# Normalised rows turned by matmuls with a diagonal, and a first weight piece in three transfers

## The reference

```python
h = rms_norm(x, g_mix)                      # x * rsqrt(mean(x*x) + 1e-5) * g
proj = h @ w_in + b_in                      # 1024 -> 1024+256+256+3*1024+2*1024
q, k, v, cb, cc, cx, ga, gc = split(proj)
y_attn = sliding_window_attention(rope(q), rope(k), v, sinks) @ w_attn_o
y_conv = (cb * causal_short_conv(cc * cx, w_conv)) @ w_conv_o
x = x + (sigmoid(ga) * y_attn + sigmoid(gc) * y_conv) @ w_out
h = rms_norm(x, g_ffn)
x = x + moe(h)        # top 4 of 32 experts, each w_gate, w_up, w_down of 1024x1024
return rms_norm(x, g_final)
```

## Time and profile before

| | |
|---|---|
| runs | 1164.71 us median of 3 (1164.37 to 1169.08) |
| profiled execution | 1164.72 us, of which the span in the trace is 1162.9 us |
| busy share of the span | PE 96%, PE weight load 45%, DVE 31%, ACT 21%, POOL 2% |
| DMA | 447.44 MB, mean 385 GB/s over the span |
| chain that ended last | PE 69%, DMA 29% |

### The profile page before, as it was taken

How to read it: one execution, slowest core, us unless ns; L and a number is a source line. 1 busy time by engine, 2 the same in 40 slices (tenths; PEclk the granted TensorE clock), 3 DMA queues, 4 the chain that set the end, 5 groups by cost and what they waited for, 6 DMA issues and landing times.

```text
span 1162.9 us, 14215 instructions
## 1 busy us (share of the span) xinstructions
PE 1120.3 (96%) x5623; PEld 522.5 (45%) x5623; DVE 359.9 (31%) x684; ACT 238.9 (21%) x426; POOL 26.9 (2%) x59
## 2 busy tenths in 40 slices
PE   8999999999999999999999999999999999999997
PEld 7888888973333333333333333333333333333332
DVE  6988896742111121121111111111111111111111
ACT  6676765421000001000100000000000000000002
POOL 2100000000000000000000000000000000000000
PEclk9999999999999999999999999999999999999999
DMA  9455749899999999999999999999999999999995
GB/s 293 155 176 169 263 142 352 299 405 427 427 427 431 431 431 429 429 430 432 429 432 432 431 431 430 432 431 432 429 432 429 432 431 431 429 432 431 425 423 240
DMA packets 65393, 447.44 MB, mean 385 GB/s; under 512 B 4569, under 2 KB 44853, under 8 KB 46421
## 3 DMA queue, kind: packets, MB, share of 16 engines
q1 hardware_dynamic: 65088, 446.93, 92.9%
q10 hardware_dynamic: 277, 0.12, 0.0%
HBM read 445.59 MB, written 1.05 MB: 384 GB/s over the span
## 4 chain that ended last, share of the span: by engine, by line
PE 69%; DMA 29%; ACT 0%; DVE 0%; issue 0%; POOL 0%; ACTq 0%; DVEq 0%; POOLq 0%
PE psum L821 36%; DMA ring<-in_w_up 29%; PE psum L538 10%; PE psum L542 5%; PE psum L836 4%; PE psum L759 4%; PE psum L558 2%; PE psum L849 1%; PE psum L767 1%; PE psum L792 1%; PE psum L608 0%; PE psum L843 0%; PE psum L598 0%; PE psum L524 0%; PE psum L865 0%; PE psum L652 0%
## 5 line engine op out<-in xcount | busy, mean ns | idle before, releaser
L821 PE MATMUL psum<-ring,work 128*64 128x512 f32 x3072 | 694.9, 602 | 29.0 <-DMA ring<-in_w_up 28.5
L821 PEld LDWEIGHTS psum<-ring,work 128*64 128x64 f32 x3072 | 217.4, 138 | 456.3 <-issue 404.1
L1512 DVE TENSOR_SCALAR work<-psum 128x512 f32<-128x512 f32 x32 | 22.1, 692 | 280.7 <-PE psum L821 280.7
L538 PE MATMUL psum<-hh,w 128*128 128x512 f32 x384 | 97.4, 395 | 0.0
L1256 DVE TENSOR_TENSOR w<-ring,w 128x1024 fp32r<-128x1024 f32 x74 | 90.4, 1264 | 8.4 <-ACT w L1005 8.1
L1517 DVE TENSOR_SCALAR work<-psum 128x512 f32<-128x512 f32 x32 | 22.1, 692 | 205.7 <-PE psum L821 205.7
L1165 ACT COPY work<-psum 128x512 f32<-128x512 f32 x32 | 18.8, 587 | 311.2 <-PE psum L849 311.1
L1005 ACT CAST w<-ring 128x1024 fp32r<-128x1024 f32 x74 | 74.2, 1048 | 28.3 <-PE psum L542 15.2
L538 PEld LDWEIGHTS psum<-hh,w 128*128 128x128 f32 x384 | 68.9, 189 | 15.0 <-ACT w L1005 1.3
L1535 DVE TENSOR_TENSOR work<-psum,g2k 128x256 f32<-128x256 f32 x62 | 23.4, 419 | 165.5 <-PE psum L767 165.5
L1174 ACT ACTIVATE work<-work 128x512 f32<-128x512 f32 x32 | 20.2, 630 | 225.9 <-DVE work L1512 225.9
(11 more groups left out here) (210 smaller groups left out, 687.9 us busy)
## 6 DMA issues: line engine op xcount, KB each, us to landing
ring<-in_w_gate SPq DMA_DIRECT2D x25, 4096.0 KB, 39.7
ring<-in_w_up SPq DMA_DIRECT2D x25, 4096.0 KB, 37.2
ring<-in_w_down SPq DMA_DIRECT2D x25, 4096.0 KB, 39.9
ring<-in_w_gate SPq DMA_DIRECT2D x13, 2048.0 KB, 12.9
ring<-in_w_up SPq DMA_DIRECT2D x13, 2048.0 KB, 12.5
ring<-in_w_in SPq DMA_DIRECT2D x25, 1024.0 KB, 5.0
ring<-in_w_down SPq DMA_DIRECT2D x8, 2048.0 KB, 13.1
ring<-in_w_down SPq DMA_DIRECT2D x10, 1024.0 KB, 35.6
```

The lines of the kernel that those rows point to most:

```text
L538: pe.matmul(bank(b[m]).rearrange("p (x t) -> p x t", x=2), wH[:, par, m, k, :], both[:, :, k, :], start=(k == 0), stop=(k == KB - 1))
L821: mm = pe.matmul(psum[64 * h:64 * h + 64, b, :], src[:, k, :], w[:, k2, h * 512:(h + 1) * 512], start=(bias_of is None and k == 0), stop=( ...
```

## The change

What it does, part by part:

- `normed` is no longer made for the first norm. VectorE multiplies the 128 x 128 identity by 1/rms instead, once for each tile of tokens (`diag`), and TensorE multiplies the blocks of x itself by that diagonal: one float32 matmul both scales and turns a block. Five blocks (`LEAD`) of the first tile go ahead of the wait for the second diagonal; the other three stand between blocks of the second tile.
- `WARM` goes from 3 to 2.
- The first weight piece comes in three transfers (blocks 0 and 1, 2 and 3, 4 to 7), with a semaphore more.
- Its blocks 0 and 1 are rounded by VectorE ahead of the first `hL`, 2 and 3 by GpSimd ahead of 4 to 7; ScalarE rounds none of them.

```diff
-WARM = 3
+WARM = 2
+LEAD = 5
@@ names
+        diag = work[:, 0:TT * P].rearrange("p (t c) -> p t c", t=TT)
@@ SyncE
-            for half, full in enumerate((first_in, piece_full[0])):
-                ks = slice(4 * half, 4 * half + 4)
+            for k0, k1, full in ((0, 2, first_in), (2, 4, second_in), (4, KB, piece_full[0])):
+                ks = slice(k0, k1)
@@ TensorE, turn_normed
-                for t in range(TT):
-                    for k in range(KB):
-                        if k % 2 == 0:
-                            pe.wait_ge(normed_ready, 4 * t + k // 2 + 1)
-                        tr = pe.transpose(turned(k)[:, t * P:(t + 1) * P], normed[:, t, k * P:(k + 1) * P], ident)
-                        if t == TT - 1 and (k == 0 or k % 2):
-                            tr.then_inc(done, 1)
+                def scaled(t, k):
+                    return pe.matmul(turned(k)[:, t * P:(t + 1) * P], xres[:, t, k * P:(k + 1) * P], diag[:, t, :],
+                                     start=True, stop=True)
+
+                pe.wait_ge(diag_ready, 1)
+                for k in range(LEAD):
+                    scaled(0, k)
+                pe.wait_ge(diag_ready, 2)
+                for k in range(KB):
+                    tr = scaled(1, k)
+                    if k == 0 or k % 2:
+                        tr.then_inc(done, 1)
+                    if k + LEAD < KB:
+                        scaled(0, k + LEAD)
@@ ScalarE
-            act_e.wait_ge(first_in, 16)
-            nc.scalar.copy(*first_weights(0, 2)).then_inc(first_high, 1)
@@ VectorE
-                for quarter in range(4):
-                    at = slice(quarter * PW, (quarter + 1) * PW)
-                    v.tensor_scalar(normed[:, t, at], xres[:, t, at], small[:, 4 + t:5 + t], None, ALU.mult).then_inc(normed_ready, 1)
-                    if t == 0 and quarter == 0:
-                        mean_rows_in(1)
+                v.tensor_scalar(diag[:, t, :], ident, small[:, 4 + t:5 + t], None, ALU.mult).then_inc(diag_ready, 1)
                 if t == 0:
+                    mean_rows_in(1)
...
             dve.wait_ge(par_ready, 1)
+            dve.wait_ge(first_in, 16)
+            v.tensor_copy(*first_weights(0, 2)).then_inc(first_high, 1)
             for k in range(KB):
-                if k == 2:
-                    dve.wait_ge(first_in, 16)
-                    v.tensor_copy(*first_weights(2, 4)).then_inc(second_high, 1)
@@ GpSimd
+            pool.wait_ge(second_in, 16)
+            g.tensor_copy(*first_weights(2, 4)).then_inc(second_high, 1)
             pool.wait_ge(piece_full[0], 16)
```

More of the change, by code:

```diff
@@ L258, in hybrid_block @@
         quarter_full, quarter_used = sem("quarter_full"), sem("quarter_used")
-        first_in, second_high, rest_high = sem("first_in"), sem("second_high"), sem("rest_high")
+        first_in, second_in, second_high, rest_high = sem("first_in"), sem("second_in"), sem("second_high"), sem("rest_high")
         x_in = [sem(f"x_in{t}") for t in range(TT)]
@@ L266, in hybrid_block @@
         dve_step, act_step, pool_step = sem("dve_step"), sem("act_step"), sem("pool_step")
-        ssq_ready, ms_ready, rstd_ready, normed_ready = (sem("ssq_ready"), sem("ms_ready"), sem("rstd_ready"),
-                                                         sem("normed_ready"))
+        ssq_ready, ms_ready, rstd_ready, diag_ready = (sem("ssq_ready"), sem("ms_ready"), sem("rstd_ready"),
+                                                       sem("diag_ready"))
         par_turned, par_ready, x_turned, hT_ready = sem("par_turned"), sem("par_ready"), sem("x_turned"), sem("hT_ready")
```

## The result

The changed kernel takes 1167.57 us (median of 14 runs, 1165.65 to 1172.40); the kernel before, 1165.88 us (14 runs, 1163.95 to 1169.68). The ratio is 1.0023, 95% interval 1.0014 to 1.0032: slower by about 2.7 us (the two medians alone lie 1.7 us apart), where I had forecast 0.25 us, but within the 0.5% that I called no change.

| | spans, mean of n | largest span | outside the span, median |
|---|---|---|---|
| before (118 runs beside the experiments) | 1163.5 | 1166.8 | 1.85 |
| changed (22 runs) | 1165.7 ± 0.4 | 1169.6 | 2.7 |

What follows compares the result with a forecast made beforehand. TensorE was taken to bound the first 60 us, DMA of expert weights to set the pace from about 579 us. Span 1162.9 + 0.25 for TensorE's shift + 1.82 around it gave 1165.0 us, range 1163.8 to 1167.8.

Steps and rivals of the forecast that it cites:

- rival 2: TensorE's clock rises before 6.9 us, blocks end at 10.8, first product starts at 10.9; 1164.4 us; chance 0.2.
- The rival of four transposes' price: A float32 matmul of 128 columns costs four transposes, 0.44 us; first product 2.6 us later, 1167.6 us; chance 0.05.
- my 2.2: Ratio of a float32 block's estimated price to a transpose's, 0.24 / 0.109 us, at the upper clock.
- 6.40 us: End of the two idle matmuls at the start, instead of 8.11 us with three.
- I put the rise at 8.2: TensorE's clock goes up at 8.2 us, so about three blocks cost 0.43 us and the others 0.24.
- the late one: Rival: clock stays low through the blocks, 1167.5 us, or 1170.5 if the first product runs low too; chance 0.15.
- the sum: TensorE's shift from 16.95 us on: earlier start -1.4, longer blocks +2.5, gap -0.45, first product -0.4; +0.25 us.
- 1.82 around it: Time outside the span, taken from the profiled execution of the kernel before and added unchanged: 1.82 us.
- I take this factor as one: A shift of TensorE in the first 17 us moves the end by the same amount; lower end nought.
- My scatter: Allowance of 0.35 us in the range for the runs before, whose lower two lie 0.34 us apart.
- The chances: Whole kernel against a bound of 0.5% or 5.8 us: same 0.97, slower 0.02, faster 0.01.

Runs made afterwards that it cites:

- e15: The changed kernel with no edit, one single profiled execution; span 1167.7 us.
- e6: The kernel before with two idle matmuls at the start instead of three; ratio 0.9998 to the kernel before, mean span 1162.9 us.
- e8: The changed kernel with transposes of x for the diagonal's float32 matmuls, scaling by 1/rms left out; ratio 1.0002 to the kernel before, mean span 1163.2 us.
- e5: The changed kernel with transfers and weight rounding taken back, leaving the diagonal and two idle matmuls; ratio 1.0021 to the kernel before, mean span 1165.4 us.
- e3: The changed kernel with three idle matmuls at the start instead of two; ratio 1.0029 to the kernel before, mean span 1166.0 us.
- e9: The kernel before with sixteen more transposes of zeros behind the real ones; ratio 1.0010 to the kernel before, mean span 1165.0 us.
- e10: The changed kernel with one more idle float32 matmul of 256 columns in TensorE's pause; ratio 1.0014 to the kernel before, mean span 1164.7 us.
- e4: The kernel before with the three transfers and moved weight rounding, transposes and three idle matmuls kept; ratio 1.0005 to the kernel before, mean span 1163.3 us.

## Why the prediction was wrong

*The first 17 us were right in their pieces.* Start of the blocks 6.9 (measured 6.90), second diagonal 8.15 (8.04), 0.24 us for a float32 block (3.91 / 16 = 0.244), no gap, 3.85 us for the first product (3.86), both casts and the third transfer hidden. But I had the blocks end at 11.3 and the V piece at 17.1 to 17.3; it was 10.8 and 16.67, the very times of rival 2, since the clock was up sooner than my 8.2 us. The rival of four transposes' price (0.44) falls: from start to start a block takes 0.223 us with the clock up, and a transpose 0.109, so it costs two transposes (my 2.2 set an estimate for a chain row against a distance of starts). One row I misread: the weight load at 5.34 us is the fifth of L608's six, not the fourth; the fourth matmul starts there, and so 6.40 us stands.

*The step that failed first is the clock's: "I put the rise at 8.2".* I took one execution's rise as the kernel's, and gave the late one a chance of 0.15. In six profiles with the diagonal and the pause (two idle matmuls, then nothing until the first diagonal) it was late twice: blocks of 5.88 and 6.32 us, V piece at 18.67 and 19.11. The transposes before cost 1.9 us in the earlier trace rows and never more than 2.6 in any profile of this study. At the low clock the change has twice as much TensorE work in that stretch to lose (a block takes 0.43 us in e15, a transpose 0.213 in e6). The six V pieces average 17.59, against 16.66 in six profiles of kernels with the old blocks and three idle matmuls: 0.9 us later, where the sum had 0.25. (0.7 of it are the two late ones, 0.2 the other four, which average 16.94.)

*The second is the sum's last term: "1.82 around it".* I carried it over as a constant. It became 2.7 us, and small edits of GpSimd's or VectorE's program move it by 0.5. It was in none of my rivals.

*The third is open: "I take this factor as one".* Of the 2.2 us in the span 0.9 are accounted for by the V pieces; the remaining 1.3 ± 0.6 are seen in no single profile. The diagonal's matmuls carry all of it (e8 takes 2.5 us away, e5 alone has 1.9). A shift does reach the end, but e3, e9 and e10, whose V pieces are 1.4, 0.8 and 0.6 us later than 16.66 in their profiles, have mean spans 2.5, 1.5 and 1.2 us longer, each more than its shift; e4, e6 and e8, which start 0.4, 0.6 and 0.5 earlier, gain 0.2, 0.6 and 0.3. The granted clock recorded with every run points at one place to look: its mean is 0.9862 in the 22 runs of the changed kernel and 0.9871 in the 118 of the kernel before, and the changed kernel's seven runs at 0.985 have a mean span of 1167.4, its nine at 0.987 or 0.988 one of 1164.2. As this record reads 1.00 through the first 12 us even in e15, the difference lies later: more or longer stretches of low clock, such as those at 380 us (about 1 us) or behind the last wait (1.7 us). An estimate from the means, 0.0009 of 1164 us, is 1.1 us. No run tests this, nor why a later start should bring them; the cause stays open.

*The base was off as well.* 1164.71 was the median of three runs; of fourteen it is 1165.88, and of 118 spans the mean is 1163.5, not the 1162.9 from which I summed. My scatter allowed 0.35 us for this and needed 1.2. The measured 1167.57 lies inside my range, 1163.8 to 1167.8, but by luck: the upper end was made for an execution with a late clock, and what filled it is the base, the time outside the span and a part that I hadn't thought of. The sum was +0.25 us and the kernel lost 2.7.

*The chances* (no change 0.97, slower 0.02) were right as to 0.5%; the interval ends at 0.32%.

## What to carry to other kernels

A matmul that also scales is not free because it saves another engine's work: here a float32 matmul of 128 columns cost two float32 transposes with the clock up (0.223 us against 0.109), and 0.43 us with it low, so put it where TensorE has been busy, or where TensorE isn't the chain. Where a small edit is at stake, don't take the clock's rise, the time around the span or a stretch of low clock from one profiled execution; time the kernel before ten times or more, and split each time in the span and the rest. Ask of every late stretch whether a later wait still takes it up: here 1.4 us lost at 383 us cost nothing, a loss of 3 us there about 1 us, and 1.7 us at 1082 us all of it.

## What the runs showed of the hardware

- The granted clock reads 1.00 in the first 8 us, while an instruction of the same form takes 0.86 us a piece there and 0.46 us later; in e15 it reads 1.00 up to 12 us, while the blocks' instructions are 0.213 us apart and then 0.112. The column can't be used for the start; the distance of the instructions can.
- In this kernel a long stretch of low clock shows as a slow DMA: the slice at 380 us reads 402 to 416 GB/s in the seven profiles with a granted clock of 0.66 to 0.71 there, and 424 to 431 in the other 13.
- A single instruction more on GpSimd changes the time outside the span by 0.5 us (1.86 to 2.36), and six fewer on VectorE, with six waits fewer on TensorE, by 0.45, with spans that stay within their errors.
- Of six executions with the same two idle matmuls, the same pause of 0.3 to 0.6 us and the same blocks behind, two had the blocks at the low clock for most of their length and four hardly or not at all: the same program meets the clock at different points.
